# Reordering the join from the first feed-forward block into the mixing block: token tile 0's last products, sums and transposes

## What is computed

```python
x = x + 0.5 * swiglu(rms_norm(x, ffn1_norm[l]), ffn1_w1[l], ffn1_w3[l], ffn1_w2[l])   # D_FF = 2816
h = rms_norm(x, mix_norm[l])
z = h @ w_in[l]                                                                      # 1024 x 6752
...                       # three attention-like branches, gates, w_out, a second swiglu
```

## Time and profile before

| | |
|---|---|
| median of 3 runs | 1601.87 us (1601.13 to 1605.47) |
| profiled execution, its own time | 1601.64 us |
| its span, first to last instruction | 1599.8 us |
| PE busy | 1579.1 us (99%) |
| DVE, ACT, POOL busy | 1061.3, 826.8, 261.2 us |
| granted TensorE clock, mean | 0.999 of full speed |

### The profile page before, as it was taken

The page is one execution under the profiler, slowest core; times in us unless marked ns, Lnnn a source line. Parts: engine busy times, 40 slices in busy tenths (PEclk is TensorE's granted clock), DMA queues, the critical chain, the costliest instruction groups (busy, mean ns, idle before and its releaser), DMA issues.

```text
span 1599.8 us, 27273 instructions
## 1 busy us (share of the span) xinstructions
PE 1579.1 (99%) x11244; PEld 1434.4 (90%) x11244; DVE 1061.3 (66%) x1267; ACT 826.8 (52%) x1127; POOL 261.2 (16%) x207
## 2 busy tenths in 40 slices
PE   9999999999999999999999999999999999999998
PEld 9999888898989999999988889998999898879886
DVE  5555657866865555655565777576555589978996
ACT  5443446653454343543455766345344475757574
POOL 0000061010000000000015001000000049704960
PEclk9999999999999999999999999999999999999999
DMA  7657555443456656556746543354656457146612
GB/s 254 219 186 229 182 185 172 132 139 106 164 179 196 199 184 198 180 187 200 230 158 193 159 152 125 113 186 157 211 184 207 142 192 230 34 140 203 219 34 93
DMA packets 207813, 273.99 MB, mean 171 GB/s; under 512 B 18822, under 2 KB 168168, under 8 KB 207208
## 3 DMA queue, kind: packets, MB, share of 16 engines
q1 hardware_dynamic: 207576, 272.67, 52.9%
q10 hardware_dynamic: 144, 0.00, 0.0%
HBM read 271.61 MB, written 1.08 MB: 170 GB/s over the span
## 4 chain that ended last, share of the span: by engine, by line
PE 90%; DVE 6%; ACT 2%; issue 1%; POOL 0%; POOLq 0%; ACTq 0%; DVEq 0%
PE bank L571 30%; PE bank L620 14%; PE bank L1063 9%; PE bank L1052 7%; PE bank L2124 4%; PE bank L1256 3%; PE bank L2102 3%; PE bank L2376 3%; PE bank L1338 2%; PE bank L2277 1%; PE bank L1198 1%; PE bank L1034 1%; PE bank L1171 1%; DVE wlo L483 1%; PE bank L1138 1%
## 5 line engine op out<-in xcount | busy, mean ns | idle before, releaser
L483 DVE TENSOR_TENSOR wlo<-raw,whi 128x2048 fp32r<-128x2048 f32 (+1 forms) x255 | 575.7, 2261 | 306.3 <-ACT whi L472 305.9
L472 ACT ACTIVATE whi<-raw 128x2048 fp32r<-128x2048 f32 (+2 forms) x257 | 482.9, 1882 | 284.8 <-PE bank L620 102.2
L571 PE MATMUL bank<-hT_hi,whi 128*128 128x256 f32 x1408 | 390.9, 278 | 0.3 <-DVE wlo L446 0.3
L571 PE MATMUL bank<-hT_lo,whi 128*128 128x256 f32 x1408 | 389.6, 277 | 0.0
L571 PE MATMUL bank<-hT_hi,wlo 128*128 128x256 f32 x1408 | 389.4, 277 | 0.0
L571 PEld LDWEIGHTS bank<-hT_hi,whi 128*128 128x128 f32 x1408 | 264.3, 188 | 0.9 <-DVE wlo L446 0.5
L571 PEld LDWEIGHTS bank<-hT_lo,whi 128*128 128x128 f32 x1408 | 265.0, 188 | 0.0
L571 PEld LDWEIGHTS bank<-hT_hi,wlo 128*128 128x128 f32 x1408 | 264.4, 188 | 0.0
L620 PE MATMUL bank<-whi,Y 128*128 128x512 f32 (+1 forms) x748 | 224.2, 377 | 0.0
L620 PEld LDWEIGHTS bank<-whi,Y 128*128 128x128 f32 x748 | 140.2, 188 | 28.0
L326 POOL TENSOR_TENSOR st<-st 128x1 f32<-128x1 f32 x17 | 14.0, 834 | 917.4 <-ACT X L319 917.4
(11 more groups left out here) (410 smaller groups left out, 2834.4 us busy)
## 6 DMA issues: line engine op xcount, KB each, us to landing
raw<-in_ffn_w SPq DMA_DIRECT2D x131, 1024.0 KB, 5.3
raw<-in_w_in SPq DMA_DIRECT2D x80, 1024.0 KB, 5.2
raw<-in_w_out SPq DMA_DIRECT2D x16, 1024.0 KB, 4.8
raw<-in_w_br_na SPq DMA_DIRECT2D x4, 1024.0 KB, 5.1
raw<-in_w_br_mla SPq DMA_DIRECT2D x4, 1024.0 KB, 5.0
raw<-in_w_br_gla SPq DMA_DIRECT2D x4, 1024.0 KB, 5.0
raw<-in_cmp_k_w SPq DMA_DIRECT2D x4, 1024.0 KB, 5.1
raw<-in_cmp_v_w SPq DMA_DIRECT2D x4, 1024.0 KB, 5.7
```

The source lines that it names most:

```text
L472: act.activation(m["whi"][:, slot, 0:w], m["raw"][:, slot, 0:w], ACT.Copy).then_inc(s.hi_ready, 1)
L483: dve.tensor_tensor(m["wlo"][:, slot, 0:w], m["raw"][:, slot, 0:w], m["whi"][:, slot, 0:w].bitcast(F32), ALU.subtract).then_inc(s.lo_ready, 1)
L571: mm = pe.matmul(B[bank][:, mt * T:(mt + 1) * T], a, b, start=(n == 0 and k == 0), stop=(n == KK - 1 and k == 2))
```

## The change

It changes three lines of the tables and nothing else: no instruction is added, except that `lo.1` becomes one instruction of 2048 columns in place of two of 1024. Loads keep their order. `lo.1`, which stood ahead of and between the tile's remainders in two halves, goes behind `hl.0-3`, and `add.3` goes behind `hl.4`.

```diff
 PE1 = words("""
-    dn.0-2 dn.4-5 dn.3 dn.6-7 xt.0 pk.0-6 xt.1 pk.7-15 proj.1-3 small gq kr gk gla_up lat proj.4 na_turn.0-1 proj.5 score.0
+    dn.0-1 dn.4-5 dn.2-3 dn.6 xt.0 dn.7 pk.0-7 xt.1 pk.8-15 proj.1-3 small gq kr gk gla_up lat proj.4 na_turn.0-1 proj.5 score.0
...
 ACT1 = words("""
-    hi.0 hidh sq.0 hi.1 hh.0-5 sq.1 hh.6-7 hi.2 hh.8-15 hi.3 proj.0 hi.4-5 proj.1 hi.6-7 proj.2 hi.8-9 proj.3 hi.10 small
+    hi.0 hidh sq.0 hi.1 hh.0-6 sq.1 hh.7 hi.2 hh.8-15 hi.3 proj.0 hi.4-5 proj.1 hi.6-7 proj.2 hi.8-9 proj.3 hi.10 small
...
 DVE1 = words("""
-    hidl lo.0 add.0-1 scale.0 add.2 lo_a.1 hl.0-3 add.3 lo_b.1 hl.4-5 scale.1 hl.6-15 lo.2-4 proj.0-1 lo.5-9
+    hidl lo.0 add.0-1 scale.0 add.2 hl.0-3 lo.1 hl.4 add.3 hl.5-6 scale.1 hl.7-15 lo.2-4 proj.0-1 lo.5-9
```

## The result

| | before | after |
|---|---|---|
| median of 22 runs each | 1604.12 us (1600.55 to 1605.68) | 1607.51 us (1604.25 to 1613.46) |
| ratio, 95% interval | | 1.0023 (1.0017 to 1.0030) |
| span of the profiled execution | 1599.8 us | 1603.5 us |
| first `dn` to first matmul of `proj.1`, both joins | 25.01, 25.03 us | 26.85, 26.87 us |

The change makes the kernel 0.23% slower, clear of the noise of the runs, though under the 0.3% named in the prediction. The forecast was +3.76 us or 0.23%; measured are +3.39 us between the medians (0.21%, inside the interval) and +3.7 us between the two profiled spans.

The account below looks back on a forecast made before the run. PE, busy 99% of the span, was taken as the bound. Its waits per join rise from 1.33 to 3.21 us, +1.88, over two joins +3.76, giving 1605.6 us; range 1601.8 to 1607.4, 8 in 10.

Parts of the forecast that it names:

- the 0.3% named in the prediction: Whole run: about 0.3%, 4.8 us, is what a measurement of this kernel can tell from no change.
- PE's five terms: PE's waits per join at `dn.4`, `pk.4`, `pk.5`, `pk.7` and `pk.8`: 3.21 us in sum, against 1.33 before.
- The new wait at `dn.4`: On PE, `dn.4` in third place waits for `hidl` on DVE: 0.85 us, 0.93 with the refill.
- The wait before `pk.7`: On PE, `pk.7` waits for `hl.7`, which stands behind `scale.1` on DVE: 1.14 us, 1.22 with the refill.
- That what follows the joins moves along: After each join, the mix is driven by PE's own progress and carries the join's delay on to its end.
- The step "against the median of the runs shown, 0.23 higher, 1605.6 us": Whole program: puts the forecast 0.23 us above 1605.4, the figure from the profiled execution, giving 1605.6 us, 0.23% more.
- the range given: Whole program: 1601.8 to 1607.4 us, said to hold 8 in 10.
- The gain (1): In the joins, `dn.7` covers the first remainder, nothing new appears, all 1.33 us goes: 1599.2 us; 5 in 100.
- the smaller change (2): In the joins, one of two new waits is smaller or absorbed later: 1601.9 to 1603.8 us; 20 in 100.
- Rival 3: On DVE, `lo.1` takes 2.75 us and `lo.2` ends after PE wants `proj.1`: 1607.5 us; 15 in 100.
- The clock: PE's pauses in the joins put the array back to half clock: 11.0 us in all, 1616.6 us; 2 in 100.

Follow-up runs that it names:

- experiment 1: Changed kernel with `hidh` ahead of `hi.0` on ScalarE, nothing else; join 25.93 us against 26.85, ratio to the kernel before 1.0010.
- (5): Kernel before with `hidh` ahead of `hi.0` on ScalarE, nothing else; join 25.02 us against 25.01.
- experiment 2: Changed kernel with `add.3` ahead of `lo.1`, `scale.1` behind `hl.6` and `sq.1` ahead of `hh.6`; join 26.09 us against 26.85.
- 3: Changed kernel with `xt.1` back between `pk.6` and `pk.7` on TensorE, nothing else; join 25.99 us against 26.85.
- experiment 6: Changed kernel, early half kept: `hidh` first, `add.3` between `lo.1` halves, `sq.1`, `scale.1` and `xt.1` moved earlier; join 24.75 us, ratio to before 0.9998.
- the kernel with PE's order alone: TensorE's changed order with the orders of VectorE and ScalarE of before; join 25.97 us against 25.01 before.

## Why the prediction came out as it did

**The mechanism was right, step by step.** In the first join (predicted, measured): `dn.4` 185.54, 185.54; `xt.0` 192.45, 192.47; `pk.0` 194.69, 194.72; `hl.0` 193.51, 193.56; `lo.1` 194.89, 194.94; `pk.4` 197.65, 197.62; `add.3` 197.42, 197.40; `pk.5` 198.58, 198.54; `scale.1` 200.01, 199.98; `pk.7` 201.18, 201.14; `xt.1` 201.95, 201.91; `pk.8` 203.27, 203.22; `proj.1` 208.85, 208.81. None of these is off by more than 0.05 us. Further off are `hi.1` (191.25, measured 191.35) and `hh.0` (193.10, measured 193.18), where the working also goes on with 193.10 though 191.25 + 1.82 is 193.07. PE's five terms, in the order of the sum, were 0.93, 0.29, 0.24, 1.22 and 0.53; by starts they measure 0.93, 0.23, 0.23, 1.22 and 0.52.

**The new wait at `dn.4`** was priced at 0.93 us and measured at 0.92 by taking away its cause (experiment 1, read from the joins), with the control that the same edit is worth nothing before (5).

**The wait before `pk.7`**: that it comes from `add.3` behind `lo.1` and `hl.4`, by way of `scale.1`, is shown by experiment 2, in which `sq.1` moved along. That PE's order makes it worse, since `pk.7` and `xt.1` both wait in turn, is shown by 3. The three mends share their gains: each of them alone wins 0.76 to 0.92 us and all three, with `lo.1` in halves again, win 2.10.

**The size.** Forecast +3.76 us, 0.23%; measured ratio 1.0023 (1.0017 to 1.0030). That what follows the joins moves along was right as well: from the first matmul of `proj.1` in one join to the first `dn` of the other lie 607.75 us before and 607.94 after.

**What failed is the base.** The step "against the median of the runs shown, 0.23 higher, 1605.6 us" took the median of three runs, 1601.87, for the level of the kernel. In 22 runs, these three among them, that level is 1604.12, 2.25 us higher; two of the three are the second and third lowest of the 22. The same sum on it gives 1604.12 + 3.76 = 1607.9; measured is 1607.51, 0.11 us above the top of the range given, 1607.4. The range held the unknown costs of the edit, and had nothing for the level: the three runs shown spread over 4.3 us themselves (1601.13 to 1605.47), more than the whole effect. Why the level lay lower in the three is not settled. The level also differs between sets of runs: on the chip of experiment 1 the same kernel's median was 1603.08 in 21 runs, and on that level the same sum gives 1606.8, inside the range. That the profiled spans differ by 3.7 us, so close to 3.76, owes something to luck too: single executions of one kernel differ by more than that.

The prediction also said that a measurement could tell only about 0.3% from no change. With 22 runs each the interval is 0.07% to either side of 0.23%, so a slowdown of this size is seen.

**The rivals.** The gain (1) and the smaller change (2) are refuted by the join times. Rival 3 asked for 2.75 us in `lo.1` and a `lo.2` that ends too late; `lo.1` took 2.28, the value chosen, and `lo.2` was over at 207.81, a microsecond before `proj.1`. The reason given for 2.28, that POOL does nothing at that time, is not borne out: in the changed kernel `lo.2` and `lo.3` run while POOL works and take 2.34 and 2.29. Timelines of DVE and POOL:

```profile
205.47 2.34 DVE L483 TENSOR_TENSOR wlo<-raw,whi 128x2048 fp32r<-128x2048 f32 x1
208.27 2.29 DVE L483 TENSOR_TENSOR wlo<-raw,whi 128x2048 fp32r<-128x2048 f32 x1 [0.47 <-ACT whi L472]
```

```profile
203.03 8.09 POOL L1902 TENSOR_TENSOR X<-Y,consts 128x256 f32<-128x256 f32 x6 [3.08 <-PE bank L353]
```

What made the one row of 2.75 before so long stays open.

**The clock** did not fall. Stretches of the changed kernel (length, busy PE, PEld, DVE, ACT, POOL, granted clock, DMA share, GB/s):

```profile
182.00:193.00 11.00, 10.31 (x50) 8.30 (x49) 6.24 (x8) 5.23 (x5) 0.54 (x1) 1.00 0.59 191
193.00:209.00 16.00, 14.75 (x69) 11.34 (x68) 11.61 (x22) 9.94 (x21) 6.52 (x7) 1.00 0.22 68
```

PE pauses for 1.25 of 16 us there and is granted its 2.4 GHz level throughout (1.00 in both rows); PE's longest pause there is 0.97 us in the brackets. The Trainium skill ("TensorE: Matmul & The Clock Gate", "HAM oscillation — how this bites in real kernels") describes a kernel whose array falls back to half clock at each wait for DMA between its groups of products; no run here shows it behind pauses as short as these.

## What to carry to other kernels

When a step is moved up in an in-order queue, look at the start of each of its inputs before anything else: here a step was moved up by 1.37 us to an input that was over only 0.66 us before the step's old place, and with the 0.14 us from the input's end to the start 0.85 us became a wait. An instruction that heads a long way round (sum of squares, power, scale) must not stand behind a long one that nobody needs yet; cutting the long one in two lets it through and costs under 0.1 us here (2 x 1.13 us by starts, against 194.94 to 197.13, 2.19, for the whole). The cut was not tried by itself in the changed kernel, only within the kernel of experiment 6. And the effect of a local edit can be forecast to a few hundredths of a microsecond from starts in a trace, while the absolute level of a kernel, taken from three runs, can't: state the difference, and give the level its own uncertainty.

## What the runs showed that was not expected

In one execution a stretch that no edit touches took a few per cent longer with no fall of the granted clock. The chain of the changed kernel, and that of the kernel with PE's order alone, over the same 168 products of L1063 behind the first join (start, length, what):

```profile
392.23 19.25 PE bank L1063 x168
```

```profile
391.96 19.99 PE bank L1063 x168
```

The second is 3.8% longer; both have a granted clock of 1.00 from 389 to 412. The time is spread over the stretch and is no single pause: most products start 0.12 us after the last one, where in the changed kernel most start 0.11 after it. In the other nine profiled executions this piece takes 19.24 to 19.27 us in both layers, and so it does in the second layer of this one. From the first `proj.1` to the second join's first `dn` that execution takes 609.95 us, against 607.75 and 607.94 in the kernels before and after. What slowed the products is open. Such stretches are a reason to compare the kernels by their joins.
